# Attention loops of a two-block kernel: chunk ends, key loads and the GQA maxima are moved and reshaped

## What is computed

```python
def gqa_attend(q, k, v):            # 16 query heads on 4 key heads, head width 64
    s = jnp.einsum('bqhgd,bkhd->bhgqk', q, k).astype(jnp.float32) * (GQA_HEAD_DIM ** -0.5)
    p = jax.nn.softmax(s, axis=-1).astype(v.dtype)
    return jnp.einsum('bhgqk,bkhd->bqhgd', p, v)

def mla_attend(q_nope, q_rope, k_nope, k_rope, v):   # 16 heads, width 64 + 32
    s = (jnp.einsum('bqhd,bkhd->bhqk', q_nope, k_nope)
         + jnp.einsum('bqhr,bkr->bhqk', q_rope, k_rope)).astype(jnp.float32) * ((MLA_NOPE + MLA_ROPE) ** -0.5)
    p = jax.nn.softmax(s, axis=-1).astype(v.dtype)
    return jnp.einsum('bhqk,bkhd->bqhd', p, v)
```

## Time and profile before

| | us |
|---|---|
| median of 3 runs (3566.53 to 3567.2) | 3566.96 |
| profiled execution, as timed | 3564.46 |
| its span in the trace | 3562.7 |
| granted PE clock, mean of the span | 0.988 |
| GQA stage, first to last score matmul | 1813.9 to 2360.8 |
| MLA stage, first to last score matmul | 2906.8 to 3458.7 |
| PE busy over the span | 3386.1 (95%) |

### The profile page before, as it was taken

One profiled execution on the slowest core, in us unless ns is written; L12 is line 12 of the kernel. 1 busy time (PEld: TensorE's weight loads), 2 busy tenths in 40 slices (PEclk: granted clock), 3 DMA queues, 4 the chain that ended last, 5 costly groups with the idle time before them and its releaser, 6 DMA issues.

```text
span 3562.7 us, 48300 instructions
## 1 busy us (share of the span) xinstructions
PE 3386.1 (95%) x15156; PEld 2681.3 (75%) x15156; DVE 2187.2 (61%) x2655; ACT 1790.9 (50%) x3060; POOL 1534.3 (43%) x977
## 2 busy tenths in 40 slices
PE   7999999999999999899999999899988999999999
PEld 5777887778888888687876777678665667777777
DVE  6674878477575766537346666666558875555551
ACT  3343878232010101334258888861465657877870
POOL 3303444544444444510156666656210026666652
PEclk9999999999999999999999999999999999999999
DMA  2134231311212121122433443412254334232311
GB/s 100 49 117 126 62 90 55 146 38 58 89 55 87 46 96 40 52 101 107 147 85 75 94 91 71 103 65 89 98 207 148 124 108 123 54 82 53 77 42 71
DMA packets 196087, 313.54 MB, mean 88 GB/s; under 512 B 100928, under 2 KB 111680, under 8 KB 195968
## 3 DMA queue, kind: packets, MB, share of 16 engines
q1 hardware_dynamic: 195968, 312.01, 29.8%
HBM read 234.02 MB, written 77.92 MB: 88 GB/s over the span
## 4 chain that ended last, share of the span: by engine, by line
PE 68%; DVE 12%; issue 7%; ACT 6%; POOL 3%; DMA 2%; SPq 2%; DVEq 0%; ACTq 0%; POOLq 0%
PE PBX L281 10%; PE PBX L283 10%; PE PBX L282 10%; PE PMX L281 5%; PE PMX L282 5%; PE PMX L283 5%; PE PMX L1966 4%; PE PD L2007 2%; PE PD L2008 2%; PE PD L2009 2%; PE PD L868 2%; DVE gqa_m L2098 1%; PE PBX L1991 1%; PE PBX L1990 1%; PE PBX L1992 1%
## 5 line engine op out<-in xcount | busy, mean ns | idle before, releaser
L216 POOL TENSOR_TENSOR w_hi<-w_stage,zero 128x1024 fp32r<-128x1024 f32 (+2 forms) x123 | 226.9, 1845 | 1251.8 <-PE PBX L283 759.5
L2076 POOL TENSOR_TENSOR gqa_pl<-gqa_pf,gqa_ph 128x512 fp32r<-128x512 f32 (+1 forms) x288 | 371.7, 1309 | 184.9 <-ACT gqa_ph L2049 184.0
L2076 POOL TENSOR_TENSOR mla_pl<-mla_pf,mla_ph 128x512 fp32r<-128x512 f32 x256 | 351.8, 1383 | 205.8 <-ACT mla_ph L2049 201.6
L2098 DVE TENSOR_REDUCE gqa_m<-PMX 128x1 f32<-128x1280 f32 (+1 forms) x158 | 200.9, 1272 | 168.7 <-PE PMX L1966 168.0
L218 POOL TENSOR_TENSOR w_lo<-w_stage,w_hi 128x1024 fp32r<-128x1024 f32 (+2 forms) x123 | 300.1, 2440 | 9.7
L1691 ACT ACTIVATE conv_in<-PBX 128x512 f32<-128x512 f32 x66 | 39.5, 600 | 480.7 <-PE PBX L283 476.7
L2098 DVE TENSOR_REDUCE mla_m<-PMX 128x1 f32<-128x1280 f32 x126 | 187.4, 1487 | 87.6 <-PE PMX L1966 87.2
L2044 ACT ACTIVATE mla_pf<-PBX 128x512 f32<-128x512 f32 x320 | 189.8, 593 | 97.2 <-PE PBX L1992 87.3
L2044 ACT ACTIVATE gqa_pf<-PBX 128x512 f32<-128x512 f32 (+1 forms) x352 | 201.8, 573 | 52.9 <-PE PBX L1995 48.6
L2049 ACT ACTIVATE gqa_ph<-gqa_pf 128x512 fp32r<-128x512 f32 (+1 forms) x352 | 215.6, 613 | 13.8
L281 PE MATMUL PBX<-ffn_hi,w_hi 128*128 128x512 f32 x528 | 206.8, 392 | 3.8 <-DVE ffn_lo L665 3.8
(11 more groups left out here) (415 smaller groups left out, 9978.4 us busy)
## 6 DMA issues: line engine op xcount, KB each, us to landing
mod_w<-in_w_mod SPq DMA_DIRECT2D x48, 512.0 KB, 3.5
w_stage<-in_w_up SPq DMA_DIRECT2D x44, 512.0 KB, 3.5
w_stage<-in_w_go SPq DMA_DIRECT2D x24, 512.0 KB, 3.7
gqa_k<-kh_d SPq DMA_DIRECT2D x32, 320.0 KB, 4.9
gqa_q<-qh_d SPq DMA_DIRECT2D x32, 320.0 KB, 7.6
w_stage<-in_w_down SPq DMA_DIRECT2D x24, 384.0 KB, 3.0
qh_d<-heads_qh SPq DMA_DIRECT2D x32, 256.0 KB, 2.0
ql_d<-heads_ql SPq DMA_DIRECT2D x32, 256.0 KB, 2.3
```

The costliest lines, as they stand in the source:

```text
L216: pool.tensor_tensor(w_hi[s][:, 0:st.cols], w_stage[s][:, 0:st.cols], z, ALU.add).then_inc(w_hi_done, 1)
L2076: eng.tensor_tensor(self.PL[k % 4][:, 0:n], self.PF[k % 4][:, 0:n], self.PH[k % 4][:, 0:n].bitcast(F32), ALU.subtract).then_inc(self.lo_dv ...
L2098: dve.tensor_reduce(self.M[g % 2][:, t:t + 1], MX[:, 0:w], AX.X, ALU.max, negate=True)\
```

## The change

1. **Chunk ends later.** `run` takes a lag for each engine. ACT's `rden` stays 3 steps behind for long chunks and is 5 behind for the context chunk; DVE's `final` is 5 behind for long chunks and 7 for the context chunk. PE's `values` stay 3 behind.
2. **Loads split.** Keys and the rounded queries (`load_k`, `load_q`) are loaded as soon as the scores of the buffers' former head have ended; the remainder of the queries (`load_q_lo`) and the values (`load_v`) still wait for its `values`. The first maxima of a head wait for keys and queries alone, the values have a semaphore of their own (`v_and_const`), which `values` of a head's first step waits for. MLA gets this too.
3. **GQA maxima on 64 rows.** The maxima used all 128 rows: on rows 0 to 63 the rounded keys, on rows 64 to 127 their remainder, against the rounded queries twice. Now each matmul has 64 rows, the rounded keys alone, and the 512-column pieces of a tile alternate between rows 0 to 63 (`K[0]`) and rows 64 to 127 (`K[1]`, whose keys now lie there). For that the operand with the maxima's row is rearranged: rows 0 to 63 of `K[1]` are ones, rows 0 to 63 of `Q[1]` zero but for row 0, which is the maxima's, so its score matmul has 128 rows. DVE clears these rows of `Q[1]` once for each buffer.

```diff
@@ head_buffers, __init__
-            kr, qr = ((97, 96), (97, 96)) if layout == "mla" else ((P, 65), (P, 65))
+            kr, qr = ((97, 96), (97, 96)) if layout == "mla" else ((P, P), (P, P))
-                self.load_inc = 16 * (6 if self.mla else 8)
+                self.load_inc = 16 * (4 if self.mla else 6)
@@ run
-                    for k in range(self.LAG, self.SB + self.LAG):
+                    for k in range(lag, self.SB + lag):
                         if k < self.SB or not last:
                             step(i + k // self.SB, k % self.SB, last)
-                        finish(i, k - self.LAG)
+                        finish(i, k)
+            def ended(self, finish, i, k, long_lag, ctx_lag):
+                for lag, ctx in ((long_lag, False), (ctx_lag, True)):
+                    x = k - lag
+                    if x < self.SB and self.steps[x][4] and (self.steps[x][1] == 2) == ctx:
+                        finish(i, x)
@@ load_kv, load_q
-                    parts = [(K[0][0:64, :], kh), (K[0][64:128, :], kl), (K[1][0:64, :], kh)]
+                    parts = [(K[0][0:64, :], kh), (K[0][64:128, :], kl), (K[1][64:128, :], kh)]
@@ const_dve
+                ones_rows = self.K[q][0][96:97, :] if self.mla else self.K[q][1][0:64, :]
+                dve.memset(ones_rows.bitcast(F32), 1.0).then_inc(self.v_and_const[q], 1)
+                if not self.mla:
+                    dve.memset(self.Q[q][1][0:64, :].bitcast(F32), 0.0).then_inc(self.v_and_const[q], 1)
@@ maxima
-                        mm = pe.matmul(MX[:, s - lo_:e - lo_], self.Q[q][0][0:mr, o:o + P], self.K[q][0][0:mr, s:e],
+                        half = 0 if self.mla else (s - lo_) // C % 2
+                        rows = slice(64 * half, 64 * half + self.dim)
+                        mm = pe.matmul(MX[:, s - lo_:e - lo_], self.Q[q][0][rows, o:o + P], self.K[q][half][rows, s:e],
@@ values
+                    if first and c == 0:
+                        pe.wait_ge(self.v_and_const[q], i * 32 + self.const_n)
@@ act, dve
-                self.run(act, step, lambda i, k: rden(i, k) if self.steps[k][4] else None)
+                self.run(act, step, lambda i, k: self.ended(rden, i, k, self.LAG, self.LAG + 2), self.LAG + 2)
-                self.run(dve, step, lambda i, k: final(i, k) if self.steps[k][4] else None)
+                self.run(dve, step, lambda i, k: self.ended(final, i, k, self.LAG + 2, self.LAG + 4), self.LAG + 4)
```

More of the change, by code:

```diff
@@ L1804, in __init__ @@
                 self.mla = layout == "mla"
-                self.row = 96 if self.mla else 64
+                self.row = 96 if self.mla else 0
                 self.K, self.Q, self.V = zip(first, head_buffers(name, scope, 1, layout, chunks[-1][0] + chunks[-1][1]))
@@ L1815, in __init__ @@
                 self.nq = chunks[-1][0] + chunks[-1][1]
-                self.load_inc = 16 * (6 if self.mla else 8)
-                self.const_n = 3 + (32 if self.mla else 0)
-                self.const = [sem(f"{name}_const{q}") for q in range(2)]
+                self.load_inc = 16 * (4 if self.mla else 6)
+                self.const_n = 32 + (35 if self.mla else 4)
+                self.v_and_const = [sem(f"{name}_v_and_const{q}") for q in range(2)]
                 self.RD = scope.sb(f"{name}_rd", [64, C])
@@ L1866, in tasks, with run @@
                 return res
-            def run(self, eng, step, finish):
-                for k in range(self.LAG):
+            def run(self, eng, step, finish, lag):
+                for k in range(lag):
                     step(0, k, False)
                 def body(i, last):
-                    for k in range(self.LAG, self.SB + self.LAG):
+                    for k in range(lag, self.SB + lag):
                         if k < self.SB or not last:
                             step(i + k // self.SB, k % self.SB, last)
-                        finish(i, k - self.LAG)
+                        finish(i, k)
                 pairs(eng, HEADS // 2, body)
+            def ended(self, finish, i, k, long_lag, ctx_lag):
[3 more added lines that the diff above has]
+                        finish(i, x)
             def wait_lo(self, eng, i, k):
@@ L1902, in load_q @@
             def load_q(self, sp, q, h):
                 Q, r = self.Q[q], self.dim
[L1904 to L1907, removed]
+                qh = qh_d[bass.ds(h * r, r), 0:self.nq]
+                for to in [Q[0][0:r, :]] + ([] if self.mla else [Q[0][64:128, :]]):
+                    sp.dma_start(to.bitcast(F32), qh).then_inc(self.loaded[q], 16)
@@ L1909, in const_sp, with load_q_lo @@
+            def load_q_lo(self, sp, q, h):
+                r = self.dim
+                lo = 0 if self.mla else 64
+                sp.dma_start(self.Q[q][1][lo:lo + r, :].bitcast(F32), ql_d[bass.ds(h * r, r), 0:self.nq])\
+                  .then_inc(self.loaded[q], 16)
             def const_sp(self, sp, q):
                 for a, d in enumerate((krh_d, krl_d)):
-                    sp.dma_start(self.K[q][a][64:96, :].bitcast(F32), d).then_inc(self.const[q], 16)
+                    sp.dma_start(self.K[q][a][64:96, :].bitcast(F32), d).then_inc(self.v_and_const[q], 16)
@@ L1913, in const_dve @@
             def const_dve(self, dve, q):
[L1914 to L1917, removed]
+                dve.memset(self.V[q][0][:, :, 64:128].bitcast(F32), 1.0).then_inc(self.v_and_const[q], 1)
@@ L2022, in step @@
                     scores(i, k)
-                self.run(pe, step, values)
+                self.run(pe, step, lambda i, k: values(i, k - self.LAG), self.LAG)
             def act(self, act):
@@ L2270, in l0g_sp @@
         def l0g_sp(sp):
-            gqa.load_kv(sp, 0, 0)
+            gqa.load_k(sp, 0, 0)
+            gqa.load_v(sp, 0, 0)
             gqa.load_q(sp, 0, 0)
+            gqa.load_q_lo(sp, 0, 0)
             gates1.sp(sp)
@@ L2641, in qg_sp @@
             st = STREAM["l1_qg"]
-            mla.load_kv(sp, 0, 0)
+            mla.load_k(sp, 0, 0)
+            mla.load_v(sp, 0, 0)
             mla.const_sp(sp, 0)
```

31 lines of the change are left out of this document (20 added, 11 removed).

## The result

The changed kernel takes **3582.56 us** (median of six runs, 3578.29 to 3587.67), the one before in the same job 3567.08 (six, 3559.8 to 3570.77). The ratio is 1.0052 (95% interval 1.0043 to 1.0062): slower, 53 us above the forecast and outside its range. The profiled run took 3580.06, its span is 3578.2 at a granted clock of 0.991, so the clock isn't the reason.

The account below looks back on a forecast made before the run. It took DVE's in-order wait for ACT's reciprocal, delaying reductions and so PE's maxima, as the bound, ACT second. GQA -26, MLA -12, clearing +1: 3564.5 - 37 = 3527.5, plus 2.5 between median and profiled execution: 3530 us, range 3500 to 3563.

Parts of the forecast that it names:

- The chunk's end in MLA: Late ends in MLA: 0.2 of a 0.56 us stall a chunk stays, 0.38 x 32 = -12 us.
- reduction 1.49, remainder 0.69 to 1.15, end 1.54: DVE's work in MLA between two reductions' starts, 3.7 to 4.2 us; next reduction 0.3 to 0.8 late.
- The chunk's end in GQA: Late ends in GQA: two stalls of 1.3 us a head at the maxima go, 2.6 us a head.
- late reductions 0.4: GQA: DVE's reduction may be late at a chunk's end, 0.2 us twice a head, 0.4 lost.
- `values` of a head's first step: GQA: a new wait for the bank of the last head's chunk 1, 0.5 us once a head.
- The loads: Split loads end the wait ahead of a GQA head's first maxima, -0.6 us a head.
- The halves: GQA maxima on 64 rows: 1.7 us a head gained, 2.4 paid for 20 shape changes, net +0.7.
- the restart, 0.12: Price of one shape change, from PE's restart at 2011.40, where weights aren't loaded ahead: 0.13, taken as 0.12 us.
- the bound of 0.28: Upper bound for one shape change: 0.12 us plus 0.16 for the matmul in flight to end first.
- Slower: Rival, chance 0.12: each shape change costs 0.28 us, GQA loses 26 us, 3582 in all.
- Dearer changes: Rival, chance 0.15: each shape change costs 0.2 us, GQA wins nothing, 3556 in all.
- The moved stall: Rival, chance 0.10: late ends only move the stall, to `values`, reductions and MLA's `bcast` (0.5 us there), 3566 in all.

Follow-up runs that it names:

- e7: e4 with the first product of a chunk's end written to the chunk's own PSUM bank, so MIX has one SBUF operand: 3534.48 us, ratio 0.9916.
- e4: The changed kernel with the GQA maxima on 128 rows again, late ends and split loads kept: 3569.71 us, ratio 1.0016 to the kernel before.
- e6c: e4 with POOL computing 8 columns of each remainder and filling the other 504 with zeros: 3501.88 us (one run).
- e2: The kernel before with the split loads alone: 3548.61 us, ratio 0.9965.
- e3: The kernel before with the GQA maxima on 64 rows alone: 3576.55 us, ratio 1.0040.
- e1: The kernel before with the later chunk ends alone: 3578.13 us, ratio 1.0040.
- e11: The changed kernel with all three maxima matmuls of a GQA tile on rows 0 to 63: 3609.56 us (one run).

## Why the prediction was wrong

**What bounded the kernel: right.** DVE's in-order wait for ACT did delay the reduction behind it; with the late ends `t` waits for ACT 3.9 us in all instead of 63.9.

**The chunk's end in MLA: wrong, and the larger error.** The step that failed is the walk "reduction 1.49, remainder 0.69 to 1.15, end 1.54", then "a diagonal of 0.7". The end took 3129.77 - 3127.56 = 2.2 and the diagonal 1.41, so DVE is later by 0.7 + 0.7 = 1.4 us than I had it, and `bcast` waits 1.4 where I had 0 to 0.5. 30 times 1.4 is 42 us; minus the maxima's stall, which did go (0.56 x 32 = 18), it leaves 24, and the stage shows 22. I had seen a remainder at 1.23 beside others at 0.69 and carried that spread for the remainder alone. The MIX and the diagonal are the same kind of instruction, and their short time held only where the kernel before had put them. e7 shows the cause: one operand moved, MIX at 0.69, and MLA gains 24.8 us where 12 were forecast.

**The chunk's end in GQA: wrong for the same reason.** Of two stalls a head, 2.6 us, I counted both as gone. One stayed:

```profile
2008.38 1.49 DVE L2150 TENSOR_TENSOR MIX<-gqa_t,gqa_gate 64x512 f32 x1
2009.90 1.49 DVE L2126 TENSOR_REDUCE gqa_m<-PMX 128x1 f32<-128x1280 f32 x1
```

```profile
2011.44 0.61 PE L1992 MATMUL PMX<-gqa_k,gqa_q 64*128 64x512 f32 x3 [0.66 <-DVE gqa_m L2126]
```

With MIX at 0.69 the reduction would start 0.8 us earlier, and PE's 0.66 would not be there. Without halves GQA came to 33.3 us a head (e4) for the 32.0 forecast, and e6c gave 31.95. The term "late reductions 0.4" was the one mis-sized; by this difference it is 1.7. A part of it is the chunk's diagonal: PE waits for it 11.3 us in e4's GQA, 5.0 in the kernel before, where the prediction took this wait as unchanged.

**`values` of a head's first step**: forecast 0.4 to 0.5 us, measured 0.28 in the timeline (4.0 us for 15). Right in kind, small in size.

**The loads: right in kind, too large in the sum.** No wait for a DMA is left ahead of a head's maxima, and the gate's late place cost nothing. But the 0.6 a head was one head's wait taken for all: in the kernel before, waits for a DMA ended PE's idle time 6 times in GQA's 16 heads, 3.0 us in all. By itself this part wins 6.7 us in GQA (e2), where 10 were forecast, and some 2.5 in MLA, which had no term in the sum; the rest of e2's 16 us isn't shown to be the loads'.

**The halves: right in sign, too cheap by the change, and near in sum by chance.** Ten tiles with two changes each at 0.12 gave 2.4 - 1.7 = +0.7. A change costs 0.19: 3.7, and by the two tile readings 8 x 0.16 + 2 x 0.37 = +2.0 us a head on PE. Half of it shows, (546.5 - 531.0)/16 = 0.97 (0.76 in e3); PE's idle time in the stage is 9 us shorter than in e4, 0.6 a head, which is about the half that doesn't. So the forecast +0.7 nearly hit because a price too low and a hidden part that the sum didn't have cancelled each other. The halves are not what made the forecast miss. The step that was mis-sized is the price's nearest row: the restart, 0.12, holds only the weights that aren't loaded ahead, while the bound of 0.28 also held the drain, and the truth is between. Of the page that I had set against it, TensorEngine Tiling (Array Packing) of the Trainium skill, section Key Properties, both statements fit: tiles of one mode run together (3 ns apart), and the first weights of the new shape begin to load 0.316 us behind the start of the matmul ahead (2004.306 to 2004.622), where in a stream it is 0.003.

**The rivals.** "Slower" was priced at 3582, and the median is 3582.6, but that is chance. Its reason, 0.28 us a change, would cost 3.9 us a head, 62 in all, and leave MLA 12 us faster; the halves cost 13 us and MLA is 22 slower. "Dearer changes" had the right price. The moved stall had the right place, `bcast` in MLA, with a third of the size. None had the shared cause.

The parts don't add up exactly. Alone they are +14, -16 and +12 us, +10 in all, and together +15.5; the difference is of the size of their intervals. In MLA most of it is the clock: with the time lost at the lower level taken out, the stage is 22.5 us longer with the late ends alone (e1) and 22.3 in the changed kernel.

## What to carry to other kernels

Before an instruction is moved, look at what its partner on the shared SBUF ports does at the new place: DVE's durations with two SBUF operands are durations of a place, and a spread of one group (0.69 and 1.23) is the sign. Keeping one operand in PSUM frees such an instruction, if nobody is in a hurry for the bank; and when a new wait of PE appears, look at the granted clock beside it. Here a pair of matmuls of another row shape among full ones saved 0.23 to 0.26 us and paid 0.4 for the way in and out. By these numbers two pairs in a row would about break even; no run has that.

## What was not expected of the hardware

- A wait can be worth something. DVE's wait for ACT had put all 64 long MIX and most of the diagonals (57 of 80) outside POOL's remainders. The late ends took 60 us of that waiting away in GQA, and DVE was held by POOL instead: it is busy for 2247.1 us in e4 and for 2158.2 in e6c, with the same instructions.
- `tensor_scalar` over 128 columns, with only its matrix and one number a row to read, is held by POOL too: 287 and 955 ns. The same section of the Trainium skill (SBUF — State Buffer, "Who interferes with whom") counts it among the forms that can take the shared ports; I had weighed only the number of SBUF operands.
- Two matmuls on different row halves start 3 ns apart, but the third comes 0.335 us later and not 0.234, and the second matmul after the tile is late by the same once more. This part isn't the other half's: in e11, where all three are on the same rows, it is the second that comes 0.34 later (2004.05 to 2004.39), and the third is at 0.23 again. It isn't the shape's either: in the kernel before, without any change of shape, the second matmul after the stall at 2011.40 comes 0.34 later too. In all of these the first weights load only when their own matmul starts (in the changed kernel at 2004.622 for 2004.624), in a stream 0.23 us ahead. So of the 0.19 us of a change some 0.08 are the way to the first matmul (0.318 for 0.234) and 0.10 the start behind it.
